# Three PSUM banks for the ring of transposes in attention, and one for the summed values

## The chip, the cores and the metric

One NeuronCore of a Trainium2 chip runs the whole program. The metric is the device time of one execution in microseconds, as the median of the runs. Engines are named as in the profile: PE or TensorE does matmuls and transposes, DVE is VectorE, ACT is ScalarE, POOL is GpSimd, SP issues most DMAs. TensorE writes only into PSUM, which has eight banks of 128 partitions x 512 fp32 here; VectorE and ScalarE carry results out of it.

## The reference

Two layers of a decoder over 1024 tokens of width 1024, all in float32. Each layer projects the normed input into four groups of four heads of width 64 and runs a different attention in each group; then comes an output projection and a mixture of experts:

```python
oa = causal_block_attention(qa, ka, va)                 # dense causal, blocks of 128 queries
ob = dilated_attention(...)                             # three dilated windows, merged
oc = causal_block_attention(qc, kc, vc, cum)            # dense causal plus summed forget gates
od, _ = banded_attention(qd, kd, vd, 127, 1, slopes, sink)   # window of 128, a sink per head
h = x + concatenate([oa, ob, oc, od]) @ w_o
return h + hierarchical_moe(rmsnorm(h, norm2_g), ...)
```

Every one of the four is a softmax over masked logits, `p = exp(s - max) / sum`, times the values. Only this part, the attention stage, concerns the change.

## The kernel before

A layer is four stages that follow one another: `project`, `attend`, `out_route` and `experts`. `attend` works on 8 pairs of heads. Pairs 0 to 5 (groups A, B, C) see all earlier keys and have six steps each: k=0 holds query blocks 0 and 1, k=1 blocks 2 and 3, k=2 to 5 one block each, 4 to 7. Pairs 6 and 7 (group D, windowed) have four steps of two blocks with at most two key blocks each. A step has one item for each head and query block, and an item has one 128x128 square of weights for each key block: 6, 14, 10, 12, 14 and 16 squares in the six steps of an unwindowed pair, 6 or 8 in a windowed one.

Each engine runs its own program over the steps in a hand-written order, tied to the others by counting semaphores. In the text, iteration p.k is the pass of the main loop (L935 on TensorE) for step k of pair p. In it:

- TensorE computes the logits two steps ahead (L880, for pairs 4 and 5 also L886) into banks 0 to 3, transposes the squares of weights of this step (L897, up to four to a bank, called a group), multiplies the values of the step before (`values`, L914), and, in some iterations, spreads the inverted denominators of a half over 64 rows (`spread_norm`, L859), spreads summed gates (`spread_cum`, L848) and transposes the next pair's queries and keys (`transpose_heads`, L839).
- VectorE adds the mask to the logits two steps ahead and takes the maximum (the max pass, L1042), inverts the denominators (L1070), copies every second group of transposed weights to SBUF (L1058), copies the transposed heads (L1017), and normalises a half (`normalise`, L1075): the summed values times the spread inverses.
- ScalarE copies the other groups (L979), takes the exponentials of the step two ahead (L971), and copies the spread inverses (`norm_out`, L986). In the windowed pairs it also takes the exponentials of the sinks (L992), which VectorE adds to the denominators (L1067).
- GpSimd scales the heads of the next pair (L814, L822) once those of this pair are transposed.

Groups of weights, spread inverses, spread gates and transposed heads all go through one ring of PSUM banks, written down in advance by `plan_ring`: entry n uses bank 4 + n % RING, and TensorE's `take` waits until entry n - RING has been copied out, by the engine that the plan names for it. With RING = 2 these are banks 4 and 5. Banks 6 and 7 hold the summed values O, the query blocks 0 to 3 (the first half) in bank 6 and 4 to 7 in bank 7. `values` of steps k=0 and k=2 wait until the same half of the pair before is normalised. VectorE normalises the first half of a pair at the end of iteration p.3 and the second at the end of iteration p+1.1:

```python
                if st.k == 3:
                    normalise(st.pair, 0)
                if st.k == 1 and st.pair > 0:
                    normalise(st.pair - 1, 1)
```

The inverses for them are spread one iteration earlier, at p.2 and p+1.0, which is what `norm_at` lists. The weights of three steps have buffers (`slot`), the transposed weights of two (`pT`).

Of the kernel before, what the change touches and what calls it, by code (L numbers as in the profile page):

```python
# [29 lines left out]
P = 128  # L30
EPS = 1e-6
NEG = -1e30
HD = 64
HEADS = 4
# [214 lines left out]
def bcast(ap, shape):  # L249
    return ap.to_broadcast(shape)  # L250
# [352 lines left out]

PAIRS = MIXERS * HEADS // 2
AHEAD = 2
RING = 2


class Item:
# [55 lines left out]
def norm_at(st):  # L665

    out = []
    if st.k == 0 and st.pair > 0:
        out.append((st.pair - 1, 1))
    if st.k == 2:  # L670
        out.append((st.pair, 0))
    return out


def cum_at(st):

    return [(st.pair + 1, st.k)] if (st.pair + 1) // 2 == 2 and st.k < 2 else []
# [44 lines left out]
def attend(nc, s, g, layer):  # L722
    NT, SEQ = s.NT, s.SEQ
    HALF = NT // 2
    bk, pm = s.banks, s.pm
# [19 lines left out]
    cum = s.cum[:, :, :]  # L745

    dilated = [bias, [s.r_proj[:, j * 1024:(j + 1) * 1024] for j in range(2)]]
    O = s.bank_pairs[3]

    def tab(st, x):  # L750
        if st.window:
# [13 lines left out]
    def step_of(pair, qb):  # L765
        return next(st for st in steps if st.pair == pair and qb in st.qbs)

    def emptied(n, who):

        return sum(w_ == who for _, _, w_ in ring[:n + 1])  # L770

    def wait_bank_empty(eng, n):
        who = ring[n][2]
        sem = g.ra if who == "a" else g.rv
        eng.wait_ge(sem.sem, sem.at(layer, emptied(n, who)))

    def ring_bank(kind, key):
        return bk[4 + ring_at[kind, key] % RING]

    def groups_done(i, who):  # L780

        n = ring_at["w", (i, len(steps[i].groups) - 1)]
        return emptied(n, who)

    with nc.Block() as block:
# [41 lines left out]
        def _(pe):  # L827
            def take(kind, key):
                n = ring_at[kind, key]
                if n >= RING:  # L830
                    wait_bank_empty(pe, n - RING)
                return bk[4 + n % RING]

# [67 lines left out]
            def values(st):  # L901
                pe.wait_ge(g.ra.sem, g.ra.at(layer, groups_done(st.i, "a")))
                if len(st.groups) > 1:
                    pe.wait_ge(g.rv.sem, g.rv.at(layer, groups_done(st.i, "v")))
                if st.k % 2 == 0 and st.k < 4 and st.pair > 0:

                    pe.wait_ge(g.on.sem, g.on.at(layer, 2 * st.pair - 1 + st.k // 2))
                for n, qb in enumerate(st.qbs):
                    two = st.items[2 * n:2 * n + 2]
                    for b in range(two[0].nb):  # L910
                        for it in two:
                            h = 2 * (st.pair % 2) + it.j
                            v0 = 384 + HD * (st.pair % 2) if st.window else 2 * GW + HD * h
                            mm = pe.matmul(O[HD * it.j:HD * (it.j + 1), qb * P:(qb + 1) * P],  # L914
                                           pm[st.m][:, it.kb0 + b, v0:v0 + HD],
                                           pT[st.i % 2][:, (it.at + b) * P:(it.at + b + 1) * P],
                                           start=b == 0, stop=b == it.nb - 1)
                mm.then_inc(g.pv.sem, 1)
# [3 lines left out]
            for i in range(AHEAD):  # L922
                logits(steps[i])
            pe.wait_ge(g.fxd.sem, g.fxd.at(layer, 3))
            ls = s.fox[:, 3]
            pe.matmul(bk[6][:, 0:NT * HEADS], s.upto[:, :], ls.rearrange("p t h -> p (t h)"),
                      start=True, stop=False)
            for t in range(NT - 1):
                left = NT - 1 - t
                mm = pe.matmul(bk[6][:, (t + 1) * HEADS:NT * HEADS], s.ones[:, :],  # L930
                               bcast(ls[:, t:t + 1, :], [P, left, HEADS]),
                               start=False, stop=(t == NT - 2))
            mm.then_inc(g.fxp.sem, 1)
# [76 lines left out]
        def _(dve):  # L1010
# [16 lines left out]
            def bias_and_max(st):  # L1027
                x = st.pair % 2
                if st.i == 0:
                    dve.wait_ge(g.causal.sem, g.causal.at(layer, 16))  # L1030
                if st.k == 0 and st.m == 1:
                    dve.wait_ge(g.dil[x].sem, g.dil[x].at(layer, 32))
                if st.k == 0 and st.window:
                    dve.wait_ge(g.win[x].sem, g.win[x].at(layer, 32))
                dve.wait_ge(g.lg.sem, g.lg.at(layer, st.i + 1))
                if st.i >= 3:

                    last = ring_at["w", (st.i - 3, len(steps[st.i - 3].groups) - 1)]
                    dve.wait_ge(g.tp.sem, g.tp.at(layer, last + 1))
                for n, it in enumerate(st.items):  # L1040
                    at = 512 * it.bank
                    nc.vector.tensor_tensor_reduce(  # L1042
                        out=weights[st.slot][:, it.at * P:(it.at + it.nb) * P],
                        in0=s.bank_pairs[it.j][:, at:at + it.nk], in1=tab(st, it), scale=1.0, scalar=3e38,
                        op0=ALU.add, op1=ALU.min,
                        accum_out=negmax[:, x, it.j, it.qb:it.qb + 1]).then_inc(g.mx.sem, 1)
                    if st.window and it.j == 1:
                        dve.wait_ge(g.mx.sem, g.mx.at(layer, items_to(st.i - 1) + n + 1))
                        nc.vector.scalar_tensor_tensor(
                            out=floor[:, x, :, it.qb], in0=s.sink_b[:, 2 * x:2 * x + 2], scalar=-1.0,  # L1050
                            in1=negmax[:, x, :, it.qb], op0=ALU.mult, op1=ALU.min).then_inc(g.nf.sem, 1)

            def weights_out(st, n):
                at, count = st.groups[n]
                dve.wait_ge(g.tp.sem, g.tp.at(layer, ring_at["w", (st.i, n)] + 1))
                if st.i >= 2:
                    dve.wait_ge(g.pv.sem, g.pv.at(layer, st.i - 1))
                nc.vector.tensor_copy(pT[st.i % 2][:, at * P:(at + count) * P],  # L1058
                                      ring_bank("w", (st.i, n))[:, 0:count * P]).then_inc(g.rv.sem, 1)

            def invert(pair, half):
                m, x = pair // 2, pair % 2
                b = slice(HALF * half, HALF * (half + 1))
                dve.wait_ge(g.ex.sem, g.ex.at(layer, items_to(step_of(pair, HALF * (half + 1) - 1).i)))
                if m == 3:
                    dve.wait_ge(g.sk.sem, g.sk.at(layer, 2 * x + half + 1))
                    nc.vector.tensor_tensor(den[:, x, :, b], den[:, x, :, b], sinkexp[:, x, :, b],  # L1067
                                            ALU.add).then_inc(g.sa.sem, 1)
                    dve.wait_ge(g.sa.sem, g.sa.at(layer, 2 * x + half + 1))
                nc.vector.reciprocal(rden[:, x, :, b], den[:, x, :, b]).then_inc(g.rd.sem, 1)  # L1070

            def normalise(pair, half):
                dve.wait_ge(g.pv.sem, g.pv.at(layer, step_of(pair, HALF * (half + 1) - 1).i + 1))
                dve.wait_ge(g.ra.sem, g.ra.at(layer, emptied(ring_at["norm", (pair, half)], "a")))
                nc.vector.tensor_tensor(mixT[:, pair, HALF * half:HALF * (half + 1), :],  # L1075
                                        bk[6 + half].rearrange("p (t n) -> p t n", n=P),
                                        r_s.rearrange("p (t n) -> p t n", n=P), ALU.mult).then_inc(g.on.sem, 1)

            dve.wait_ge(g.rt.sem, g.rt.at(layer, 1))
# [8 lines left out]
            for i in range(AHEAD):  # L1088
                bias_and_max(steps[i])
            dve.wait_ge(g.fxp.sem, g.fxp.at(layer, 1))  # L1090
            nc.vector.tensor_copy(cum, bk[6][:, 0:NT * HEADS].rearrange("p (t h) -> p t h", h=HEADS)).then_inc(
                g.fxo.sem, 1)
            for st in steps:
                if st.i + AHEAD < len(steps):
                    bias_and_max(steps[st.i + AHEAD])
                for pair, half in norm_at(st):
                    invert(pair, half)
                for n in range(1, len(st.groups), 2):
                    weights_out(st, n)
                for pair, half in cum_at(st):  # L1100
                    cum_out(pair, half)
                for pair, q in heads_at(st):
                    heads_out(pair, q)
                if st.k == 3:
                    normalise(st.pair, 0)
                if st.k == 1 and st.pair > 0:
                    normalise(st.pair - 1, 1)
            invert(PAIRS - 1, 1)
            normalise(PAIRS - 1, 1)


# [677 lines left out]
```

## Time and profile before

| | us |
|---|---|
| median of 3 runs (lowest, highest) | 2372.94 (2370.99, 2377.91) |
| the profiled execution | 2372.53 |
| its span in the trace | 2370.6 |
| TensorE's matmuls and transposes busy in the span | 2101.8 |
| VectorE, ScalarE, GpSimd busy | 701.5, 540.7, 309.6 |
| attention stage, from the first logits to the last normalise, layer 0 | 326.3 to 606.3 |

A line of the profile names the source line, the engine, the operation and the memory that it writes and reads. A timeline row gives the start and the duration in microseconds, neighbouring instructions of one line merged (x8 is eight of them), and in square brackets how long the engine stood idle before it and what ended that. PE is the matmul side of TensorE, PEld the loading of weights, which overlaps it. Matmuls with 64 rows or columns are recorded twice, so x28 on L914 is 14 matmuls.

### The profile page before, as it was taken

Reading aid. Unit: us, or ns where it says so; the run is one execution under the profiler, and the core shown is the slowest. Engines: PE = TensorE matmul, PEld = TensorE weight load, DVE = VectorE, ACT = ScalarE, POOL = GpSimd, SP = SyncE. Lnnn points to the kernel's source line nnn. Section 1 sums busy time; section 2 is a strip of 40 time slices with the busy share of each in tenths; the row PEclk is TensorE's granted clock in tenths of the full one; section 3 lists DMA queues with packets and bytes.
Section 4 is the critical chain, followed back from the end, with each engine's and each line's share of the span. In section 5 each row is a group of like instructions: output and inputs, shape, how many; then the busy total and the mean of one; then the engine's idle time right before and its main releaser. Section 6 shows DMA issues by size and latency. Waiting matters only on the chain. (4 is left out here: it accounts for less than half of the span.)

```text
span 2370.6 us, 28157 instructions
## 1 busy us (share of the span) xinstructions
PE 2101.8 (89%) x9724; PEld 1207.8 (51%) x9724; DVE 701.5 (30%) x1725; ACT 540.7 (23%) x1281; POOL 309.6 (13%) x356
## 2 busy tenths in 40 slices
PE   7999958898996899999389999688989959999992
PEld 4555536666554444444155555466664534444441
DVE  0111145545243122222411110455452332222223
ACT  1211135545211011111021211455451110111110
POOL 0221221100011000000211221201000110000002
PEclk9999979999997999999689999799999969999996
DMA  6000000020423999999610000000201229999996
GB/s 223 18 14 4 0 27 19 2 76 6 143 74 120 349 369 367 367 363 372 261 34 18 18 0 1 27 19 2 76 6 56 72 73 348 369 361 370 368 352 257
DMA packets 212770, 355.68 MB, mean 150 GB/s; under 512 B 19136, under 2 KB 162368, under 8 KB 212672
## 3 DMA queue, kind: packets, MB, share of 16 engines
q1 hardware_dynamic: 183232, 269.93, 32.5%
q0 software_dynamic: 14848, 50.36, 6.2%
q10 hardware_dynamic: 14592, 34.11, 3.6%
q8 instruction: 59, 0.97, 0.2%
q14 instruction: 39, 0.32, 0.0%
HBM read 303.88 MB, written 50.48 MB: 149 GB/s over the span
## 5 line engine op out<-in xcount | busy, mean ns | idle before, releaser
L399 PE MATMUL banks<-r_win,r_tile 128*128 128x384 f32 (+3 forms) x1536 | 531.3, 505 | 9.2 <-DMA r_win<-in_w_in 7.0
L1626 PE MATMUL banks<-r_proj 128*128 128x512 f32 x1024 | 454.3, 597 | 4.6 <-DVE r_proj L1681 4.6
L399 PEld LDWEIGHTS banks<-r_win,r_tile 128*128 128x128 f32 x1536 | 292.6, 192 | 226.6 <-issue 64.4
L1626 PEld LDWEIGHTS banks<-r_proj 128*128 128x128 f32 x1024 | 191.1, 192 | 222.5 <-issue 216.6
L1613 PE MATMUL banks<-r_proj 128*128 128x512 f32 x512 | 230.5, 593 | 3.0 <-ACT r_proj L1666 3.0
L1233 PE MATMUL banks<-r_proj 128*128 128x512 f32 x512 | 226.8, 598 | 5.2 <-DVE r_proj L1321 5.2
L897 PE MATMUL banks<-fixed,r_win 128*128 128x128 f32 x984 | 146.5, 281 | 43.7 <-ACT r_win L979 20.5
L971 ACT ACTIVATE r_win<-r_win 128x256 f32<-128x256 f32 (+7 forms) x256 | 177.2, 695 | 22.7 <-DVE r_win L1042 21.2
L897 PEld LDWEIGHTS banks<-fixed,r_win 128*128 128x128 f32 x984 | 104.6, 141 | 102.6 <-issue 70.8
L1697 DVE TENSOR_TENSOR r_proj<-r_proj,banks 128x256 f32<-128x256 f32 x64 | 26.9, 421 | 435.7 <-ACT r_proj L1662 435.7
L1233 PEld LDWEIGHTS banks<-r_proj 128*128 128x128 f32 x512 | 95.9, 191 | 116.7 <-issue 116.7
L880 PE MATMUL banks<-r_win 64*128 64x512 f32 (+3 forms) x704 | 138.3, 501 | 16.9 <-DVE r_win L1017 13.5
L1579 POOL DMA_INDIRECT r_proj<-normed,r_proj x64 | 60.0, 938 | 633.3 <-PE banks L1601 618.8
L1613 PEld LDWEIGHTS banks<-r_proj 128*128 128x128 f32 x512 | 92.6, 191 | 96.3 <-issue 92.8
L979 ACT ACTIVATE r_win<-banks 128x512 f32<-128x512 f32 (+1 forms) x148 | 84.5, 571 | 242.0 <-PE banks L897 242.0
L914 PE MATMUL banks<-r_win,r_proj 128*64 128x128 f32 x1968 | 126.6, 277 | 0.0
L1042 DVE CUSTOM_DVE_ANT_0 r_win<-banks,w_lat 128x256 f32<-128x256 f32 (+7 forms) x128 | 90.6, 755 | 96.6 <-PE banks L886 61.9
L465 ACT ACTIVATE r_proj<-banks,rx 128x384 f32 (+3 forms) x80 | 48.0, 600 | 301.1 <-PE banks L399 301.1
L914 PEld LDWEIGHTS banks<-r_win,r_proj 128*64 128x64 f32 x1968 | 105.7, 137 | 14.6 <-issue 14.1
L532 DVE TENSOR_SCALAR r_proj<-banks,rl 128x256 f32 (+1 forms) x16 | 7.7, 484 | 355.2 <-PE banks L420 355.2
L1662 ACT ACTIVATE r_proj<-banks 128x256 f32<-128x256 f32 x64 | 24.5, 383 | 375.5 <-PE banks L1626 375.5
L1601 PEld LDWEIGHTS banks<-fixed,r_proj 128*128 128x128 f32 x512 | 68.1, 192 | 65.8 <-DMA r_proj<-normed,r_proj 36.0
(165 smaller groups left out, 1780.7 us busy)
## 6 DMA issues: line engine op xcount, KB each, us to landing
r_proj<-in_w SPq DMA_DIRECT2D x192, 1024.0 KB, 9.9
expert_rows<-r_proj ACTq DMA_DIRECT2D x64, 512.0 KB, 7.3
r_win<-in_w_in SPq DMA_DIRECT2D x6, 1536.0 KB, 19.7
r_proj<-in_w_o SPq DMA_DIRECT2D x2, 4096.0 KB, 13.5
normed<-r_proj SPq DMA_DIRECT2D x16, 512.0 KB, 3.2
out<-r_tile SPq DMA_DIRECT2D x16, 512.0 KB
r_tile<-in_x SPq DMA_DIRECT2D x8, 512.0 KB, 4.1
r_win<-in_w_in SPq DMA_DIRECT2D x2, 2048.0 KB
```

Source lines behind the costliest of these rows:

```text
L399: mm = pe.matmul(bk[b][:, 0:CHUNKS[c]], uT[j][:, k, :], w_ch[c][:, k, :], start=(k == 0), stop=(k == KT - 1))
L880: mm = pe.matmul(bk[2 * it.j + it.bank + c // 512][:, 0:cw], qT[x][rows, qb * P:(qb + 1) * P], kT[x][rows, at + c:at + c + cw], start=True ...
L897: mm = pe.transpose(bank[:, b * P:(b + 1) * P], weights[st.slot][:, (at + b) * P:(at + b + 1) * P], s.ident[:, :])
L914: mm = pe.matmul(O[HD * it.j:HD * (it.j + 1), qb * P:(qb + 1) * P], pm[st.m][:, it.kb0 + b, v0:v0 + HD], pT[st.i % 2][:, (it.at + b) * P:( ...
L971: nc.scalar.activation(p, p, ACT.Exp, bias=top, scale=-1.0, accum_out=den[:, x, it.j, it.qb:it.qb + 1]).then_inc(g.ex.sem, 1)
L979: nc.scalar.activation(pT[st.i % 2][:, at * P:(at + count) * P], ring_bank("w", (st.i, n))[:, 0:count * P], ACT.Copy).then_inc(g.ra.sem, 1)
L1042: nc.vector.tensor_tensor_reduce(out=weights[st.slot][:, it.at * P:(it.at + it.nb) * P], in0=s.bank_pairs[it.j][:, at:at + it.nk], in1=tab ...
L1233: mm = pe.matmul(bk[2 * j + c][:, :], mt[j][:, k, :], s.w_o[:, k, 512 * c:512 * c + 512], start=(k == 0), stop=(k == KT - 1))
L1579: nc.gpsimd.indirect_dma_start(out=xg[e % 2], out_offset=None, in_=s.xn_dram, in_offset=bass.IndirectOffsetOnAxis(ap=idx[:, e:e + 1], axis ...
L1601: mm = pe.transpose(bk[k // 4][:, (k % 4) * P:(k % 4 + 1) * P], xs[:, k, :], s.ident[:, :])
L1613: mm = pe.matmul(bk[6 + c][:, :], hidT[j][:, k, :], w2[j][:, k, 512 * c:512 * c + 512], start=(k == 0), stop=(k == F // P - 1))
L1626: mm = pe.matmul(bk[2 + j][:, 0:2 * F], xT[j][:, k, :], w13[j][:, k, :], start=(k == 0), stop=(k == KT - 1))
```

## The change

The ring gets three banks, 4 to 6, and the summed values of both halves share bank 7. Since the two halves then use the same columns, `values` at the first step of each half waits until the half before (of this pair or the last) is normalised, and `normalise` moves to the iterations that `norm_at` names, p.2 for the first half and p+1.0 for the second, one iteration earlier than before. The small sum of the forget gates at the start goes to bank 7 too.

```diff
--- before.py
+++ after.py
@@ -603,7 +603,7 @@
 
 PAIRS = MIXERS * HEADS // 2
 AHEAD = 2
-RING = 2
+RING = 3
 
 
 class Item:
@@ -745,7 +745,7 @@
     cum = s.cum[:, :, :]
 
     dilated = [bias, [s.r_proj[:, j * 1024:(j + 1) * 1024] for j in range(2)]]
-    O = s.bank_pairs[3]
+    O = bk[7]
 
     def tab(st, x):
         if st.window:
@@ -902,16 +902,16 @@
                 pe.wait_ge(g.ra.sem, g.ra.at(layer, groups_done(st.i, "a")))
                 if len(st.groups) > 1:
                     pe.wait_ge(g.rv.sem, g.rv.at(layer, groups_done(st.i, "v")))
-                if st.k % 2 == 0 and st.k < 4 and st.pair > 0:
-
-                    pe.wait_ge(g.on.sem, g.on.at(layer, 2 * st.pair - 1 + st.k // 2))
+                if st.qbs[0] % HALF == 0 and st.i > 0:
+
+                    pe.wait_ge(g.on.sem, g.on.at(layer, 2 * st.pair + st.qbs[0] // HALF))
                 for n, qb in enumerate(st.qbs):
                     two = st.items[2 * n:2 * n + 2]
                     for b in range(two[0].nb):
                         for it in two:
                             h = 2 * (st.pair % 2) + it.j
                             v0 = 384 + HD * (st.pair % 2) if st.window else 2 * GW + HD * h
-                            mm = pe.matmul(O[HD * it.j:HD * (it.j + 1), qb * P:(qb + 1) * P],
+                            mm = pe.matmul(O[HD * it.j:HD * (it.j + 1), qb % HALF * P:(qb % HALF + 1) * P],
                                            pm[st.m][:, it.kb0 + b, v0:v0 + HD],
                                            pT[st.i % 2][:, (it.at + b) * P:(it.at + b + 1) * P],
                                            start=b == 0, stop=b == it.nb - 1)
@@ -923,11 +923,11 @@
                 logits(steps[i])
             pe.wait_ge(g.fxd.sem, g.fxd.at(layer, 3))
             ls = s.fox[:, 3]
-            pe.matmul(bk[6][:, 0:NT * HEADS], s.upto[:, :], ls.rearrange("p t h -> p (t h)"),
+            pe.matmul(O[:, 0:NT * HEADS], s.upto[:, :], ls.rearrange("p t h -> p (t h)"),
                       start=True, stop=False)
             for t in range(NT - 1):
                 left = NT - 1 - t
-                mm = pe.matmul(bk[6][:, (t + 1) * HEADS:NT * HEADS], s.ones[:, :],
+                mm = pe.matmul(O[:, (t + 1) * HEADS:NT * HEADS], s.ones[:, :],
                                bcast(ls[:, t:t + 1, :], [P, left, HEADS]),
                                start=False, stop=(t == NT - 2))
             mm.then_inc(g.fxp.sem, 1)
@@ -1073,7 +1073,7 @@
                 dve.wait_ge(g.pv.sem, g.pv.at(layer, step_of(pair, HALF * (half + 1) - 1).i + 1))
                 dve.wait_ge(g.ra.sem, g.ra.at(layer, emptied(ring_at["norm", (pair, half)], "a")))
                 nc.vector.tensor_tensor(mixT[:, pair, HALF * half:HALF * (half + 1), :],
-                                        bk[6 + half].rearrange("p (t n) -> p t n", n=P),
+                                        O.rearrange("p (t n) -> p t n", n=P),
                                         r_s.rearrange("p (t n) -> p t n", n=P), ALU.mult).then_inc(g.on.sem, 1)
 
             dve.wait_ge(g.rt.sem, g.rt.at(layer, 1))
@@ -1088,7 +1088,7 @@
             for i in range(AHEAD):
                 bias_and_max(steps[i])
             dve.wait_ge(g.fxp.sem, g.fxp.at(layer, 1))
-            nc.vector.tensor_copy(cum, bk[6][:, 0:NT * HEADS].rearrange("p (t h) -> p t h", h=HEADS)).then_inc(
+            nc.vector.tensor_copy(cum, O[:, 0:NT * HEADS].rearrange("p (t h) -> p t h", h=HEADS)).then_inc(
                 g.fxo.sem, 1)
             for st in steps:
                 if st.i + AHEAD < len(steps):
@@ -1101,10 +1101,8 @@
                     cum_out(pair, half)
                 for pair, q in heads_at(st):
                     heads_out(pair, q)
-                if st.k == 3:
-                    normalise(st.pair, 0)
-                if st.k == 1 and st.pair > 0:
-                    normalise(st.pair - 1, 1)
+                for pair, half in norm_at(st):
+                    normalise(pair, half)
             invert(PAIRS - 1, 1)
             normalise(PAIRS - 1, 1)
```

## Rows read from the trace of the kernel before

**Rows 1.** The page: busy time of each engine over the span.

```profile
PE 2101.8 (89%) x9724; PEld 1207.8 (51%) x9724; DVE 701.5 (30%) x1725; ACT 540.7 (23%) x1281; POOL 309.6 (13%) x356
```

**Rows 2.** A stretch of the attention stage: length, busy time by engine, granted clock, DMA share, GB/s.

```profile
505.00:545.00 40.00, 36.06 (x324) 24.25 (x322) 17.82 (x43) 16.71 (x42) 3.95 (x3) 1.00 0.02 8
```

**Rows 3.** What TensorE's transposes of the weights (L897) waited for, both layers: us, times.

```profile
  ACT r_win L979: 20.5, 60
  DVE r_win L1058: 20.3, 26
```

**Rows 4.** The same in layer 0 alone, from the waits of TensorE: us, times, longest.

```profile
PE banks L897 <- ACT r_win L979: 10.2, 30, 0.3
PE banks L897 <- DVE r_win L1058: 10.2, 13, 1.1
```

**Rows 5.** Timeline of iteration 1.5: start, duration, what ran, idle before and its releaser.

```profile
400.76 1.09 PE L897 MATMUL banks<-fixed,r_win 128*128 128x128 f32 x8
...
401.46 0.60 ACT L979 ACTIVATE r_win<-banks 128x512 f32<-128x512 f32 x1 [2.84 <-PE banks L897]
...
402.20 0.63 PE L897 MATMUL banks<-fixed,r_win 128*128 128x128 f32 x4 [0.34 <-ACT r_win L979]
...
403.06 0.69 DVE L1058 COPY r_win<-banks 128x512 f32<-128x512 f32 x1
...
403.87 0.42 PEld L897 LDWEIGHTS banks<-fixed,r_win 128*128 128x128 f32 x4 [1.28 <-ACT r_win L971]
403.90 0.63 PE L897 MATMUL banks<-fixed,r_win 128*128 128x128 f32 x4 [1.07 <-DVE r_win L1058]
```

**Rows 6.** Timeline of iterations 1.4, 2.0 and 2.1, TensorE.

```profile
396.53 1.14 PE L897 MATMUL banks<-fixed,r_win 128*128 128x128 f32 x6 [0.34 <-ACT r_win L979]
...
407.42 0.87 PE L897 MATMUL banks<-fixed,r_win 128*128 128x128 f32 x6
...
415.78 0.41 PE L897 MATMUL banks<-fixed,r_win 128*128 128x128 f32 x2 [0.65 <-DVE r_win L1058]
...
416.93 0.66 PE L839 MATMUL banks<-fixed,r_win 128*128 128x128 f32 x4
```

**Rows 7.** Timeline of iteration 5.4.

```profile
562.34 0.68 DVE L1058 COPY r_win<-banks 128x512 f32<-128x512 f32 x1
...
563.16 0.41 PE L897 MATMUL banks<-fixed,r_win 128*128 128x128 f32 x2 [1.03 <-ACT r_win L971]
```

**Rows 8.** Timeline of the start of the stage, layer 0.

```profile
324.63 1.61 DVE L1017 TENSOR_SCALAR r_win<-banks,gain_qk 128x512 f32<-128x512 f32 x2 [0.42 <-PE banks L839]
...
338.03 0.63 PE L839 MATMUL banks<-fixed,r_win 128*128 128x128 f32 x4 [0.56 <-ACT r_win L979]
```

**Rows 9.** Timeline of iterations 2.0 and 2.1, ScalarE and VectorE.

```profile
411.11 0.60 ACT L986 ACTIVATE r_win<-banks 128x512 f32<-128x512 f32 x1 [0.78 <-PE banks L859]
...
411.69 0.75 DVE L1017 TENSOR_SCALAR r_win<-banks,gain_qk 128x512 f32<-128x512 f32 x1 [2.17 <-PE banks L839]
...
413.19 0.96 DVE L1042 CUSTOM_DVE_ANT_0 r_win<-banks,r_win 128x768 f32<-128x768 f32 x1 [0.75 <-PE banks L880]
...
418.29 0.68 DVE L1075 TENSOR_TENSOR r_tile<-banks,r_win 128x512 f32<-128x512 f32 x1
```

**Rows 10.** Timeline of the windowed pairs, layer 0.

```profile
576.33 1.58 DVE L1017 TENSOR_SCALAR r_win<-banks,gain_qk 128x512 f32<-128x512 f32 x2 [1.90 <-PE banks L839]
...
582.32 0.93 PE L880 MATMUL banks<-r_win 64*128 64x128 f32 x8 [0.85 <-DVE r_win L1017]
...
586.58 0.60 ACT L986 ACTIVATE r_win<-banks 128x512 f32<-128x512 f32 x1 [0.37 <-PE banks L859]
...
587.65 0.42 DVE L1042 CUSTOM_DVE_ANT_0 r_win<-banks,r_win 128x256 f32<-128x256 f32 x1 [1.79 <-PE banks L880]
...
600.48 0.66 PE L897 MATMUL banks<-fixed,r_win 128*128 128x128 f32 x4
...
601.88 2.04 PE L914 MATMUL banks<-r_win,r_proj 128*64 128x128 f32 x32
```

## The prediction

> **What bounds the kernel now.** I read the page first: TensorE is busy for 89% of the span, and no other engine for more than 30% [rows 1]. The change touches the attention stage alone. A stretch of it shows TensorE busy 36 of 40 us, VectorE 18, ScalarE 17, at the full granted clock [rows 2]. So inside the stage TensorE sets the pace, with about a tenth of the time idle, and what counts is what ends its idle time. The line view gives that for the transposes of the weights: over both layers they waited 20.5 us in 60 places for ScalarE's copy out of a ring bank and 20.3 us in 26 places for VectorE's [rows 3], half of it in each layer [rows 4].
>
> The timeline shows how. In iteration 1.5 TensorE fills both ring banks from 400.76 on, eight transposes in 1.09 us, 0.137 us each. ScalarE begins its copy of the first bank 0.70 us after the fill began, takes 0.60, and TensorE resumes 0.14 later: a bank comes round in 1.44 us, and TensorE needs it after 1.09. That is the 0.34 us in front of the third group. The fourth group wants the bank that VectorE empties, and VectorE has its max passes to do first: its copy ends at 403.75, TensorE resumes at 403.90 after 1.07 us idle [rows 5].
>
> **The change, part by part.** *The third bank.* A group now waits for the group three before it. TensorE needs 3 x 4 x 0.137 = 1.64 us to come round, more than the 1.44 us of a bank that ScalarE empties, so the 0.34 us goes to zero with 0.2 us to spare. The fourth group of a step now asks for ScalarE's bank instead of VectorE's late one, and its wait goes too. What comes out in the six unwindowed pairs of a layer:
> - 30 waits for ScalarE, 10.2 us, all in these pairs (five iterations each);
> - 13 waits for VectorE, 10.2 us, of which one of 0.2 us in the last pair is counted below: 10.0 us [rows 4];
> - the fourth group of 5.4, 1.03 us. The row names the exponentials, but a copy by VectorE ends 0.14 us before it resumes [rows 7];
> - five fourth groups of x.4 that show no idle row: six transposes take 1.14 us in 1.4 and 0.87 us where nothing holds them, about 0.2 us each, 1.0 us [rows 6].
>
> That is 22.2 us a layer. Does it stay? The order of work around these waits is fixed, so I went through one unwindowed pair with the waits taken out. The max pass, the exponentials and the copies of a step are needed one or two iterations later. The tightest place is iteration x.1: after the values TensorE transposes the next pair's heads, and with a ring of three these want the bank that VectorE empties late. It came free at 415.78; TensorE reached the heads at 416.93 and will reach them 0.34 + 0.65 sooner, at 415.94 [rows 6]. Margin 0.16 us. If it were missed by 0.3 us each time, 3.6 us of the whole would return. The 0.85 us in front of the logits of each next pair stays, since it is only the heads' own way through VectorE.
>
> *The start.* The four transposed heads of pair 0 wait in the ring too: VectorE stands 0.42 us between the second and the third copy; three banks close that. The wait of 0.56 us at 338.03 goes, but the logits behind it then wait for the max pass, so 0.2 us are gained [rows 8]. Together -0.6 us a layer.
>
> *One bank for the values.* The first values of a half must now wait until VectorE has normalised the half before, so normalise (L1075, 0.68 us) moves one iteration forward, to the end of iterations x.0 and x.2, behind ScalarE's copy of the spread denominators. On VectorE the next max pass is queued behind it, and TensorE's logits wait for that. In an unwindowed pair this is covered: ScalarE's copy is done at 411.71, VectorE's heads copy ends at 412.44, normalise then ends at 413.12, and the max pass cannot start before 413.19 anyway [rows 9]. TensorE reaches the values only after fourteen transposes, 1.9 us later. Cost 0; without that cover, ScalarE's 0.60 us, VectorE's 0.68 and three hand-overs of 0.12 would stand in TensorE's way, 1.64 us a time.
>
> In the two windowed pairs the steps are short and the cover is thin [rows 10]. In 6.0, at 576.33, VectorE makes two heads copies, then normalise, and its max pass slips to about 578.3; from there it works without a pause to the copy that releases the logits at 582.32, so what TensorE saves on the way (0.45 us) is not seen: gain 0. In 6.2 and 6.3 ScalarE's copy ends at 587.18, normalise at about 587.97, and the max pass that began at 587.65 is 0.3 us late; the same again in the next pair. The lateness passes through the exponentials and the sink terms to the reciprocals for which the spreading of 7.0 waits, so the transposes at 600.48 come at 600.85 and the values at 601.88 wait for the exposed chain: 600.85 + 1.64 = 602.49. Cost +0.6 us a layer; bounds 0 and four exposed normalises, 6.6.
>
> *The rest* (the summed gates in bank 7 instead of 6) moves nothing. DMAs that wait for attention steps start earlier and have tens of us to spare; the next stage waits for the last normalise.
>
> Sum per layer: -22.2 - 0.6 + 0.6 = -22.2 us; two layers -44.4. The profiled execution took 2372.5 us, so 2328.1; the median of the runs is 0.4 us above it: 2328.5 us, 1.9% less.
>
> The sum rests on the 0.137 us per transpose of [rows 5]. The Trainium skill (TensorE: Matmul & The Clock Gate, Back-to-back issue gap) gives a sustained 81 ns for a 128-column matmul with its weight load. At that pace, an estimate, three banks would be filled in 0.97 us and a bank come round in 1.21, so a ring of three would still stall by 0.24 us in each of the 36 four-group steps, and 8.6 of the 44 us would stay. The trace disagrees with the 81 ns, and goes into the sum.
>
> **The rivals.**
> - *Part of the gain returns.* VectorE's late copies hold TensorE a little further on (the margin of 0.16 us above is small and may be negative), so that only ScalarE's waits go for good: -20.5 us, about 2352. For it: VectorE is late by over 1 us in x.5. Against: in x.5 that bank is wanted next only in the following iteration, behind the values and the next logits.
> - *The third bank does nothing.* The weight loads name the exponentials (L971) as the releaser in front of the fourth group [rows 5]. If these were the cause, the bank would not help there, and if the rate in front of ScalarE's copies were TensorE's own, nowhere: 2373. Against: the code orders the exponentials of a step two iterations ahead, and each of these waits ends 0.14 to 0.15 us after a copy out of the bank in question [rows 5, 7].
> - *Slower: the shared bank is exposed everywhere.* If every one of the 32 normalises stood in TensorE's way for its 1.64 us, 52 us would be added and 44 taken: 2381. It decides from 1.4 us each on. Against: in unwindowed pairs TensorE has 1.9 us of transposes or more in front, and ScalarE was idle before each such copy (0.78 us in [rows 9]).
>
> **How the numbers follow.** Forecast 0.80, with its own range 2324 to 2337 (the lower end if the start or the margins give 2 us a layer more, the upper one with the heads' margin missed, 3.6, and 2.5 us a layer of the windowed bound). Part returns 0.12, nothing 0.04, slower 0.03; the remaining 0.01 is faster by more. The range, 2323 to 2342, holds the forecast and the near part of the second case. A difference under 0.3% (7 us) could not be told from none: faster 0.93, same 0.04, slower 0.03.
>
> **What would show it.** In the changed profile the transposes of the weights should have next to no idle time from ScalarE's and VectorE's copies; the busy time of TensorE should be the same and the whole saving idle time; each attention stage should be 22 us shorter and every other stage unchanged. The heads' transposes in x.1 show the margin; the wait in front of the values of 7.2 should appear with about 0.5 us. I would be wrong if idle time of the same size stood in front of the values or the logits instead.

## The result

The changed kernel takes 2316.3 us in the median of 4 runs (2315.27 to 2319.48), beside 2373.26 us for the kernel before: a ratio of 0.976 with a 95% interval of 0.9742 to 0.9777. That is 57 us less. I had forecast 44 us less, 2328.5, with a range from 2323 to 2342. The direction and the place were right and the gain was put 13 us too small.

In the page of the changed kernel (as [rows 1]) TensorE's busy time has fallen too, from 2101.8 to 2087.1 us, though it executes the same 9724 instructions. I had expected it to stay the same and the whole saving to be idle time:

```profile
PE 2087.1 (90%) x9724; PEld 1209.3 (52%) x9724; DVE 697.3 (30%) x1725; ACT 541.8 (23%) x1281; POOL 309.7 (13%) x356
```

What the transposes of the weights waited for, over both layers (as [rows 3]): the two copies that made up 20.5 and 20.3 us are gone from the list, and no matmul of that line has a wait. What is left belongs to the loading of weights.

```profile
  issue: 35.7, 74
  ACT r_win L971: 1.0, 3
```

TensorE's waits in layer 0 (line, releaser, us in total, times, longest; as [rows 4]). What remains is the heads' way through VectorE, two waits at the start of the stage (one of 1.4 us for the first max pass is not shown), the reciprocals, and one new wait of 0.6 us in front of the values:

```profile
PE banks L880 <- DVE r_win L1017: 6.5, 7, 1.4
...
PE banks L859 <- DVE r_win L1070: 1.1, 3, 0.5
PE banks L880 <- DVE cum L1091: 0.6, 1, 0.6
PE banks L914 <- DVE r_tile L1075: 0.6, 1, 0.6
```

Iteration 1.5 (as [rows 5]). Sixteen transposes run in 2.06 us without a break, and the values follow 1.99 us after the first of them; before, they followed after 3.69 us. VectorE's first copy is as late as it was (it begins 2.30 us after the first transpose in both), but no transpose of weights waits for it now:

```profile
391.17 2.06 PE L897 MATMUL banks<-fixed,r_win 128*128 128x128 f32 x16
...
391.86 0.60 ACT L979 ACTIVATE r_win<-banks 128x512 f32<-128x512 f32 x1 [2.12 <-PE banks L897]
...
393.16 1.75 PE L914 MATMUL banks<-r_win,r_proj 128*64 128x128 f32 x28
...
393.47 1.28 DVE L1058 COPY r_win<-banks 128x512 f32<-128x512 f32 x2
```

Iterations 2.0 and 2.1 (as [rows 9] and the last row of [rows 6]). Normalise now stands between the heads copy and the max pass, which begins 0.15 us after VectorE has become free, as soon as the logits are there:

```profile
399.81 0.60 ACT L986 ACTIVATE r_win<-banks 128x512 f32<-128x512 f32 x1 [0.78 <-PE banks L859]
...
400.39 0.75 DVE L1017 TENSOR_SCALAR r_win<-banks,gain_qk 128x512 f32<-128x512 f32 x1 [2.17 <-PE banks L839]
...
401.06 0.68 DVE L1075 TENSOR_TENSOR r_tile<-banks,r_win 128x512 f32<-128x512 f32 x1
...
401.89 0.96 DVE L1042 CUSTOM_DVE_ANT_0 r_win<-banks,r_win 128x768 f32<-128x768 f32 x1 [0.15 <-PE banks L880]
...
403.55 0.88 PE L914 MATMUL banks<-r_win,r_proj 128*64 128x128 f32 x12
...
404.48 0.63 PE L839 MATMUL banks<-fixed,r_win 128*128 128x128 f32 x4
```

The windowed pairs (as [rows 10]). In 6.1 the max pass begins right behind normalise, in 6.2 normalise waits 1.41 us for ScalarE's copy, the logits of the next pair wait 1.44 us for VectorE instead of 0.85, the spreading of 7.0 waits 0.41 us for the reciprocals, and the values of 7.2 wait 0.55 us for normalise:

```profile
547.70 0.68 DVE L1075 TENSOR_TENSOR r_tile<-banks,r_win 128x512 f32<-128x512 f32 x1
...
548.30 0.41 DVE L1042 CUSTOM_DVE_ANT_0 r_win<-banks,r_win 128x256 f32<-128x256 f32 x1
...
552.12 0.93 PE L880 MATMUL banks<-r_win 64*128 64x128 f32 x8 [1.44 <-DVE r_win L1017]
...
557.08 0.69 DVE L1075 TENSOR_TENSOR r_tile<-banks,r_win 128x512 f32<-128x512 f32 x1 [1.41 <-ACT r_win L986]
...
569.44 1.09 PE L859 MATMUL banks<-fixed,r_win 128*64 128x128 f32 x16 [0.41 <-DVE r_win L1070]
...
572.11 1.97 PE L914 MATMUL banks<-r_win,r_proj 128*64 128x128 f32 x32 [0.55 <-DVE r_tile L1075]
```

The stage can be cut at instructions that recur in every trace. The table gives the lengths in us in layer 0 (layer 1 agrees within 0.02 in all but the first column, and one more entry, 17.83 for 17.59 in t1_wait_two), from one first instruction to the next: the first transposes of the heads; the first max pass of step 3 of pair 0; the logits issued in 0.4, 1.4, 2.4, 3.4, 4.4 and 5.4; those of 7.0 (issued in 6.2); and the first VectorE instruction of the next stage. It holds the experiments too.

| kernel | start | 0.3 to 0.4 | 0.4 to 1.4 | to 2.4 | to 3.4 | to 4.4 | to 5.4 | to 7.0 | to the end |
|---|---|---|---|---|---|---|---|---|---|
| before | 18.73 | 17.60 | 36.45 | 36.55 | 38.29 | 45.94 | 44.19 | 23.11 | 24.26 |
| after | 16.90 | 15.36 | 31.88 | 31.88 | 33.79 | 41.54 | 39.63 | 19.91 | 24.58 |
| t1_wait_two | 19.80 | 17.59 | 36.46 | 36.54 | 38.28 | 45.94 | 44.19 | 23.28 | 24.57 |
| t2_third_near | 18.06 | 16.76 | 34.15 | 34.14 | 35.90 | 43.63 | 41.90 | 20.77 | 24.58 |
| t3_fourth_near | 17.09 | 16.53 | 35.39 | 35.48 | 37.22 | 44.88 | 43.13 | 22.87 | 24.59 |
| t4_ring_two_one_bank | 19.79 | 17.61 | 36.45 | 36.54 | 38.30 | 45.94 | 44.19 | 23.28 | 24.59 |
| u0_changed_again | 18.19 | 15.36 | 31.88 | 31.88 | 33.79 | 41.55 | 39.63 | 19.92 | 24.57 |
| u1_groups_3443 | 19.19 | 15.36 | 31.78 | 31.78 | 33.64 | 41.38 | 39.53 | 19.82 | 24.58 |
| u2_first_copy_cut | 18.28 | 15.35 | 31.69 | 31.69 | 33.54 | 41.28 | 39.44 | 19.71 | 24.58 |
| u3_heads_before_values | 21.10 | 14.97 | 31.39 | 31.40 | 33.24 | 40.99 | 39.14 | 19.81 | 24.57 |

The whole stage went from 285.1 to 255.5 us in layer 0 and from 286.7 to 256.7 in layer 1, 59.6 us together; the rest of the profiled execution is 3 us longer. Over the ten traces this rest is anything from 1797 to 1803 us, so these 3 us can't be put down to the change.

### The profile page after: what moved, and what is told of

The parts are those of the page before. It is cut to its first block and busy times, and to the rows that moved or that the text cites. A ratio compares the mean times of both kernels' runs of the same rounds, so it can differ in the third digit from the quotient of the medians.

```text
span 2314.1 us, 28155 instructions
## 1 busy us (share of the span) xinstructions
PE 2087.1 (90%) x9724; PEld 1209.3 (52%) x9724; DVE 697.3 (30%) x1725; ACT 541.8 (23%) x1281; POOL 309.7 (13%) x356
## 5 line engine op out<-in xcount | busy, mean ns | idle before, releaser
L971 ACT ACTIVATE r_win<-r_win 128x256 f32<-128x256 f32 (+7 forms) x256 | 177.2, 695 | 21.7 <-DVE r_win L1042 19.5
L880 PE MATMUL banks<-r_win 64*128 64x512 f32 (+3 forms) x704 | 137.3, 498 | 18.8 <-DVE r_win L1017 14.7
L897 PE MATMUL banks<-fixed,r_win 128*128 128x128 f32 x984 | 130.7, 279 | 0.0
L897 PEld LDWEIGHTS banks<-fixed,r_win 128*128 128x128 f32 x984 | 105.6, 141 | 42.2 <-issue 35.7
## 6 DMA issues: line engine op xcount, KB each, us to landing
r_win<-in_w_in SPq DMA_DIRECT2D x6, 1536.0 KB, 20.5
```

The source lines that it names most:

```text
L880: mm = pe.matmul(bk[2 * it.j + it.bank + c // 512][:, 0:cw], qT[x][rows, qb * P:(qb + 1) * P], kT[x][rows, at + c:at + c + cw], start=True ...
L897: mm = pe.transpose(bank[:, b * P:(b + 1) * P], weights[st.slot][:, (at + b) * P:(at + b + 1) * P], s.ident[:, :])
L971: nc.scalar.activation(p, p, ACT.Exp, bias=top, scale=-1.0, accum_out=den[:, x, it.j, it.qb:it.qb + 1]).then_inc(g.ex.sem, 1)
```

## The experiments

All are edits of the changed kernel. A ratio is to the kernel before, run on the same chip, and is taken over the single runs and not from the two medians; 2373 us times the ratio gives a time that can be compared across the two sets of runs.

**Three banks, but the wait of two (t1_wait_two).**

```diff
             def take(kind, key):
                 n = ring_at[kind, key]
-                if n >= RING:
-                    wait_bank_empty(pe, n - RING)
+                if n >= 2:
+                    wait_bank_empty(pe, n - 2)
                 return bk[4 + n % RING]
```

> Three banks in the ring, but TensorE waits for the entry two before, as with two banks. If the idle time shown before the transposes is all that a bank wait costs (20.5 + 20.3 us for the two releasers and some 3 us of unlisted ones), about 44 us come back on the changed kernel's 2316.3: 2360. If every wait also costs the pipeline's emptying and refilling, some 0.2 us that the rows count as busy time, all of the gain returns: 2371 to 2375. If something other than the bank waits brought the gain (the order of normalise, the start), the time stays near 2316.

2377.8 us beside 2376.8: 0.9998 (0.9985 to 1.0012). All of the gain is gone with the waits back, as by the second reading (2371 to 2375) and not by the idle rows alone (2360). The waits in layer 0 are those of [rows 4] within 0.3 us:

```profile
PE banks L897 <- ACT r_win L979: 10.2, 30, 0.3
PE banks L897 <- DVE r_win L1058: 9.9, 12, 1.1
```

So the whole 57 us come from the waits for banks, while the idle rows of these waits in [rows 3] hold 41 of them, and 43 with the one of 5.4 in each layer.

**The near wait at the third group alone (t2_third_near).**

```diff
+                near = kind == "w" and key[1] == 2 and not steps[key[0]].window
                 if n >= RING:
                     wait_bank_empty(pe, n - RING)
+                if near:
+                    wait_bank_empty(pe, n - 2)
```

> The wait for the entry two before at the third group of a step alone, unwindowed pairs: 60 waits in the two layers. If one costs the 0.34 us of its row: +20.5 us, 2337. If one costs 0.54 us with the pipeline's emptying, less the 0.15 us that a fourth group would otherwise be held in 36 steps: 32.7 - 5.4 = +27 us, 2343.6.

0.9866 (0.9842 to 0.9891), that is 2341 us, 25 us above the changed kernel (2316 to 2317 by its own ratio), with an uncertainty of some 6. That lies between the two expectations, 2337 and 2343.6, and can't tell them apart. The table is sharper: a pair takes 34.15 us instead of 31.88, 2.27 more for five waits, where the five idle rows hold 5 x 0.34 = 1.70:

```profile
PE banks L900 <- ACT r_win L982: 10.2, 30, 0.3
```

A step of twelve transposes shows the size of one wait. With it (x8, then x4, then the values):

```profile
385.51 1.09 PE L900 MATMUL banks<-fixed,r_win 128*128 128x128 f32 x8
386.94 0.63 PE L900 MATMUL banks<-fixed,r_win 128*128 128x128 f32 x4 [0.34 <-ACT r_win L982]
387.50 1.31 PE L917 MATMUL banks<-r_win,r_proj 128*64 128x128 f32 x20
```

and without it, in the changed kernel:

```profile
381.17 1.53 PE L897 MATMUL banks<-fixed,r_win 128*128 128x128 f32 x12
...
382.62 1.31 PE L914 MATMUL banks<-r_win,r_proj 128*64 128x128 f32 x20
```

From the first transpose to the values it is 1.99 us with and 1.45 us without: the wait costs 0.54 us, of which the row calls 0.34 idle. The other 0.2 are in the busy time: eight transposes and four take 1.09 and 0.63 us in two parts and 1.53 in one. The second of the two readings holds. Five waits of 0.54 would be 2.7 us; a pair shows 2.27, since the third group's wait takes the place of a hold of 0.09 us in three of the five steps and of 0.12 us in front of the heads of x.1, both found below.

**The near wait at the fourth group alone (t3_fourth_near).** The same edit with `key[1] == 3`.

> The wait for the entry two before at the fourth group alone, 36 waits in the two layers, for VectorE's late copy. By the rows of the steps with four groups (0.34 each, 0.65, 1.07 and about 0.2 us a pair): 2.94 x 12 = +35 us, 2351. With the pipeline counted, from the group's start to the start of the values, 3.7 us a pair: +44 us, 2360; the sum of this run and the one with the third group near is then more than the whole, since a fourth group that waits for VectorE hides the wait of the third.

0.9941 (0.992 to 0.9962), that is 2359 us, 43 above the changed kernel; 2360 had been expected with the emptying of the pipeline counted, 2351 by the rows. A pair takes 3.51 to 3.60 us more in the first two periods. The waits in layer 0, and iteration 1.5:

```profile
PE banks L900 <- DVE r_win L1061: 16.3, 12, 1.6
...
PE banks L900 <- ACT r_win L974: 4.4, 6, 1.6
```

```profile
397.55 1.53 PE L900 MATMUL banks<-fixed,r_win 128*128 128x128 f32 x12
400.69 0.63 PE L900 MATMUL banks<-fixed,r_win 128*128 128x128 f32 x4 [1.60 <-DVE r_win L1061]
```

The idle time before the fourth group is 1.60 us here and was 1.07 in [rows 5], since nothing delays the third any more: the two kinds of wait hide each other, and the two runs give back 2.3 + 3.5 = 5.8 us a pair where the whole is 4.6. VectorE's late copy is the larger half.

**The second half of the change alone (t4_ring_two_one_bank).** `RING = 2`, one bank for the values, normalise early.

> Two banks in the ring, the summed values in one bank and normalise one iteration earlier: the second half of the change alone. Theory: hidden in the unwindowed pairs, 0 to 1 us a layer in the windowed ones: 2373 to 2376. Rival: sharing the bank costs some 5 us or more that the third bank pays for: 2378 or more. If moving normalise was itself a gain: 2370 or less.

1.0001 (0.9985 to 1.0016). In the table it is the kernel before in every unwindowed period within 0.01 us, and 0.17 and 0.33 us slower in the last two columns, +0.5 us a layer. (The first column has another cause, see the start below.)

**The changed kernel again (u0_changed_again).** No edit; the measure for the three that follow.

> The changed kernel once more, for comparison with the three beside it: 2316 us.

2319.1 us, 0.9774 (0.9751 to 0.9797); its periods are those of the changed kernel.

**Groups of 3, 4, 4 and 3 (u1_groups_3443).**

```diff
-        self.groups = [(g, min(4, at - g)) for g in range(0, at, 4)]
+        sizes = [3, 4, 4, 3] if at == 14 else [min(4, at - g) for g in range(0, at, 4)]
+        self.groups = [(sum(sizes[:n]), c) for n, c in enumerate(sizes)]
```

> The steps of 14 squares in groups of 3, 4, 4 and 3 instead of 4, 4, 4 and 2. Theory: with three banks the fourth group is still held by 0.14 us, since a bank comes round in 1.44 us and twelve transposes take 12 x 0.109 = 1.31; a first group of three is copied sooner, and 24 such waits go: -3.4 us, 2313. Rival (a transpose takes 0.137 us, three banks are enough): no change, 2316.

2313.4 us, 0.9753 (0.9726 to 0.978): not told apart from the changed kernel by time. The trace tells it: fourteen transposes take 1.75 us instead of 1.84, so three banks did hold TensorE, by 0.09 us and not 0.14. In 2.1 part of it returns as a wait for VectorE's copy in front of the heads (last row; 0.16 us). A pair is 0.10 to 0.16 us shorter.

```profile
391.32 1.75 PE L898 MATMUL banks<-fixed,r_win 128*128 128x128 f32 x14
...
396.17 2.06 PE L898 MATMUL banks<-fixed,r_win 128*128 128x128 f32 x16
...
409.49 0.63 PE L840 MATMUL banks<-fixed,r_win 128*128 128x128 f32 x4 [0.16 <-DVE r_win L1059]
```

**ScalarE's first copy cut short (u2_first_copy_cut).** This kernel leaves out two squares of the first copy of every step with four groups, so the values are summed over squares left from earlier steps; it shows only the time with that bank free sooner.

```diff
+                if n == 0 and len(st.groups) == 4:
+                    count = 2
                 nc.scalar.activation(pT[st.i % 2][:, at * P:(at + count) * P],
```

> ScalarE copies only two squares of the first group in the steps of four groups, so part of the transposed weights is left over from earlier steps and the values are summed over the wrong weights; the bank is free about 0.25 us sooner. Theory (the fourth group is still held by 0.14 us, 36 times): -5 us, 2311. Rival (three banks are enough): no change, 2316.

2312.6 us, 0.9745 (0.972 to 0.9769). Sixteen transposes now take 1.97 us and fourteen 1.75, so one more transpose costs 0.11 us, and every step of four groups was held by 0.09 us in the changed kernel:

```profile
387.46 1.75 PE L897 MATMUL banks<-fixed,r_win 128*128 128x128 f32 x14
...
392.30 1.97 PE L897 MATMUL banks<-fixed,r_win 128*128 128x128 f32 x16
```

A pair is 0.19 to 0.26 us shorter.

**Heads before values in x.3, with the groups 3, 4, 4, 3 (u3_heads_before_values).**

```diff
+                heads_first = st.k == 3 and not st.window
+                if heads_first:
+                    for pair, q in heads_at(st):
+                        transpose_heads(pair, q)
                 if st.i > 0:
                     values(steps[st.i - 1])
...
-                for pair, q in heads_at(st):
+                for pair, q in [] if heads_first else heads_at(st):
```

> The groups 3, 4, 4 and 3, and in the iterations x.3 the heads transposed before the values instead of after them. The wait of 0.84 us before the logits of each next pair is for VectorE's copy of these heads; the values (1.2 us) would cover part of it, until VectorE's max pass and copy that stand before it bind. Estimate 0.3 us a pair less, 12 times, on top of the groups' 3.4: 2309. Rival (VectorE is busy until then and the wait only moves): 2313.

2311.2 us, 0.9739 (0.9716 to 0.9762), the fastest kernel here. The wait before the next pair's logits is 0.51 us instead of 0.84 (last row):

```profile
386.38 0.63 PE L840 MATMUL banks<-fixed,r_win 128*128 128x128 f32 x4
386.94 1.31 PE L915 MATMUL banks<-r_win,r_proj 128*64 128x128 f32 x20
388.75 0.93 PE L881 MATMUL banks<-r_win 64*128 64x128 f32 x8 [0.51 <-DVE r_win L1022]
```

That is 0.39 us a pair beside u1 and 0.49 to 0.55 beside the changed kernel, about 6 us over the run. The times of u3 and u0 differ by 8 us with intervals that overlap, so that u3 is faster rests on the trace.

## Why the prediction was right and wrong

**Right: what bounds the stage, and that the bank waits go.** Putting the waits back in took away the whole gain (t1), and the second half of the change has no gain of its own (t4). The three rivals fell: all but some 1.5 us of the gain stayed (the heads in x.1, below), the exponentials that some rows named were not the cause, and the shared bank was not exposed in the unwindowed pairs.

**Wrong: the size of a wait, in the term "the third bank".** I took 0.137 us for a transpose, 1.09 us divided by eight, and counted as cost only the idle time of the rows. But transposes in a row start 0.11 us apart, and a single one is on record as 0.27 us long. While they follow one another, the 0.16 us by which a transpose outlasts this pace lie under the next one; before a wait they stand free, and the profile books them as busy. (Its ends of matmuls are modelled; the distances between starts are not.) In addition the first step after a wait is 0.137 us and not 0.109. In [rows 5] the third group starts 0.61 us after the last transpose of the second, where it would be 0.11: with the slower first step the wait costs 0.53 us, and its row says 0.34. [rows 6] had the pace: six transposes in 0.87 us and eight in 1.09 give 0.11 each. This is also why TensorE's busy time fell by 14.7 us; the transposes of the weights alone fell from 146.5 to 130.7.

An unwindowed pair has eight such waits (two each in x.1, x.4 and x.5, one each in x.2 and x.3). The forecast for a full pair was 5 x 0.34 + 0.65 + 1.07 + 0.2 = 3.6 us. The seven waits with an idle row cost 0.2 us each beyond it, 1.4 us. The eighth, in x.4, has no row; six transposes take 1.14 us with it and 0.88 without, and I had put 0.2 for it: 0.07 us more. Against that stand two small losses of the next paragraphs, 3 x 0.09 and 0.12 us. That makes 1.1 us more than forecast, and the second pair shows it: 36.55 - 31.88 = 4.67 us. The others gained 4.4 to 4.6. Over both layers the stage came out 15 us below the forecast: some 12 by this term (the full pairs, what is left of pair 0 and the last period before the windowed pairs) and some 3 by the start.

**Wrong in the same term: "the 0.34 us goes to zero with 0.2 us to spare".** A bank comes round in 1.44 us, as I had it, but TensorE needs it after 1.37 and not after 1.64. In iteration 1.5 of the changed kernel the thirteenth transpose starts at 392.60, 1.43 us after the first; in u2, with the bank free sooner, it starts 1.37 us after. With the slower first step behind it the hold comes to the 0.09 us that u2 gave back, in 36 steps: 3.2 us. The Trainium skill (TensorE: Matmul & The Clock Gate, Back-to-back issue gap) has 81 ns for a matmul of 128 columns in a stream, from which I had worked out a hold of 0.24 us, and set it aside for the trace. The trace has 0.110 us here, between the page's figure and my 0.137, and a hold of 0.09, between 0.24 and none. The direction of the rule was right.

**The heads in x.1.** The margin of 0.16 us was missed by 0.12. In [rows 6] TensorE had to come to the heads 0.99 us sooner, and it came 1.27 us sooner, again because the waits cost more than their rows. In 2.1 VectorE's copy out of the bank begins at 403.65 and takes 0.69 us, and the heads' transposes follow at 404.48, 0.93 us after the values instead of 0.81. It costs about 1.5 us in all.

**One bank for the values: right.** Hidden in the unwindowed pairs (t4: 0.01 us); in the windowed ones +0.5 us a layer against the +0.6 forecast, by the chain that was forecast: the max passes late behind normalise, the reciprocals of 7.0, and the values of 7.2 waiting 0.55 us.

**The start.** Forecast -0.6 us a layer, measured -1.8 and -2.2. Most of this goes with the clock and not with the change: over all traces the stretch takes 16.9 to 21.1 us, with the same instructions 16.90 in the changed kernel and 18.19 in u0, depending on when TensorE's granted clock rises. Traces in which it is at 0.50 for about the first 12 us and at 1.00 from then on can be compared; the first two lines are the kernel before, layer 0, the others the changed kernel, layer 1, each pair over the first column of the table (the granted clock is the last figure but two):

```profile
321.46:333.46 12.00, 9.64 (x36) 5.91 (x36) 4.88 (x15) 1.94 (x9) 3.94 (x3) 0.50 0.01 1
333.46:340.20 6.74, 5.89 (x41) 4.04 (x41) 4.45 (x14) 4.85 (x13) 0.00 (x0) 0.99 0.00 0
...
1470.92:1482.52 11.60, 9.35 (x36) 6.12 (x36) 4.81 (x15) 1.88 (x9) 3.94 (x3) 0.50 0.00 0
1482.52:1489.04 6.52, 5.80 (x41) 4.08 (x41) 4.40 (x14) 4.92 (x13) 0.00 (x0) 0.99 0.01 3
```

That is 18.7 against 18.1 us. Likewise, where a spell of 0.50 comes back at 14.7 us, t1 and t4 take 19.80 and 19.79 us and u1, with three banks, 19.19. So some 0.4 to 0.6 us a layer belong to the third bank (the lower figure if the 0.4 us by which the clock rose later in the kernel before cost 0.2), near the forecast.

## What to carry to other kernels

In these traces an idle row before a matmul understates what the wait costs (0.34 us of 0.54): the emptying of the pipeline before it is booked as busy. Take the pace of a stream from the difference of two lengths (eight less six), not from one length divided by its count, and the cost of a wait from the distance of the first instructions on either side of it. How many buffers are enough depends on that pace; a margin worked out with the padded one can have the wrong sign. And where two kinds of wait stand in one step, removing the earlier one alone can give less than its rows: with VectorE's waits left in (t3) a pair gained some 1.1 us, where the rows of ScalarE's hold 1.7.

## What had not been expected of the hardware

The start of the stage, where TensorE has been idle for 19 us, differs between executions of the same instructions, and the granted clock differs with it. In the changed kernel's layer 0 the logits of step 1 ran in 1.77 us and the next ones, four microseconds later, in 2.51, though the same logits take 1.35 at 394.84 us of this trace, at the full clock:

```profile
328.10 1.77 PE L880 MATMUL banks<-r_win 64*128 64x384 f32 x8 [1.43 <-DVE r_win L1042]
...
332.34 2.51 PE L880 MATMUL banks<-r_win 64*128 64x512 f32 x8 [0.59 <-DVE cum L1091]
```

The stretches of four microseconds (PEclk is the last column but two) show the granted clock at 1.00 between two spells nearer 0.50, the two levels of 2.4 and 1.2 GHz, though TensorE was busy 3.65 of the 4 us before it fell:

```profile
324.00:328.00 4.00, 1.82 (x13) 1.02 (x11) 2.66 (x10) 0.82 (x5) 3.02 (x3) 0.81 0.00 0
328.00:332.00 4.00, 3.65 (x24) 2.55 (x24) 2.12 (x9) 2.52 (x10) 0.93 (x1) 1.00 0.00 0
332.00:336.00 4.00, 3.66 (x15) 2.41 (x16) 1.39 (x6) 1.32 (x5) 0.00 (x0) 0.57 0.00 0
336.00:340.00 4.00, 4.00 (x31) 2.69 (x31) 3.33 (x9) 3.42 (x7) 0.00 (x0) 1.00 0.00 0
```

In the kernel before it was 0.50 until 332 us and 1.00 from 336 on. In layer 1 of t1_wait_two it was at 0.50 until 21.7 us after the first transposes, which is the one entry beside the first column that stands out, 17.83 us. Elsewhere the periods of the table repeat within 0.02 us between layers and between the two executions of the changed kernel, which made differences of 0.1 us a pair readable that no timing of the whole kernel could tell.
